# Selecting a head's decays with all 128 rows, and a new order of the mixer's attention products in a tick

## What is computed

```python
a_cs = jnp.cumsum(ac, axis=-1)
decay_in = jnp.exp(segsum(ac))
y_diag = jnp.einsum('bclgs,bgrcls,bcsgrp->bclgrp', cb, decay_in, xc)
```

```python
logits = jnp.einsum('bqhd,bkhd->bhqk', qi, k).astype(jnp.float32) * scale
logits = logits + ci.transpose(0, 2, 1)[..., None] - c_k[:, :, None, :]
logits = jnp.where(causal[None, None], logits, NEG_INF)
p = jax.nn.softmax(logits, axis=-1)
return jnp.einsum('bhqk,bkhd->bqhd', p.astype(v.dtype), v)
```

## Time and profile before

| | us |
|---|---|
| median of 3 runs | 2444.68 |
| lowest and highest | 2444.25, 2448.4 |
| the profiled execution, its own time | 2445.11 |
| its span | 2443.3 |
| TensorE busy (share of the span) | 2412.1 (99%) |
| VectorE, ScalarE, GpSimd busy | 1367.6, 1004.5, 403.0 |

### The profile page before, as it was taken

One profiled execution on the slowest core, in us unless ns is written; L12 is line 12 of the kernel. 1 busy time (PEld: TensorE's weight loads), 2 busy tenths in 40 slices (PEclk: granted clock), 3 DMA queues, 4 the chain that ended last, 5 costly groups with the idle time before them and its releaser, 6 DMA issues.

```text
span 2443.3 us, 30351 instructions
## 1 busy us (share of the span) xinstructions
PE 2412.1 (99%) x11930; PEld 1959.0 (80%) x11930; DVE 1367.6 (56%) x2158; ACT 1004.5 (41%) x1723; POOL 403.0 (16%) x320
## 2 busy tenths in 40 slices
PE   8899999999999999999999999999999999999998
PEld 6677877888888887788888877787788887888887
DVE  6868875763665455576456547534555445443342
ACT  5554553442444444454234334323443334332223
POOL 0342342210112222131001100001220001110011
PEclk9999999999999999999999999999999999999999
DMA  4542222223223221133332232231244322223222
GB/s 161 107 92 78 79 69 96 95 87 112 95 83 116 70 70 48 45 122 96 91 101 92 90 121 82 76 102 57 65 126 134 113 95 87 95 87 104 99 82 87
DMA packets 74269, 226.23 MB, mean 93 GB/s; under 512 B 8080, under 2 KB 12304, under 8 KB 74000
## 3 DMA queue, kind: packets, MB, share of 16 engines
q1 hardware_dynamic: 69696, 215.90, 27.5%
q10 hardware_dynamic: 4432, 8.39, 2.0%
HBM read 215.87 MB, written 8.39 MB: 92 GB/s over the span
## 4 chain that ended last, share of the span: by engine, by line
PE 59%; issue 0%; DVE 0%; ACT 0%; POOL 0%; POOLq 0%; DVEq 0%
PE bank L1142 58%; PE bank L1146 1%; ACT t L1536 0%; DVE t L1986 0%; DVE t L1993 0%; DVE t L1989 0%; ACT t L1539 0%; POOL t L2547 0%; POOLq L2768 0%; DVEq L2768 0%; DVE t L2469 0%; DVE t L2475 0%; POOLq L765 0%
## 5 line engine op out<-in xcount | busy, mean ns | idle before, releaser
L1142 PE MATMUL bank<-t 128*128 128x512 f32 (+4 forms) x11412 | 2381.7, 374 | 21.1 <-DVE t L1986 10.2
L1142 PEld LDWEIGHTS bank<-t 128*128 128x128 f32 (+1 forms) x11412 | 1903.7, 185 | 458.0 <-issue 91.1
L1536 ACT ACTIVATE t<-t 128x1024 fp32r<-128x1024 f32 (+5 forms) x649 | 549.6, 856 | 680.2 <-PE bank L1142 275.6
L1986 DVE TENSOR_TENSOR t<-t 128x1024 fp32r<-128x1024 f32 (+6 forms) x686 | 627.6, 925 | 252.3 <-ACT t L1536 247.3
L2547 POOL TENSOR_TENSOR t<-t 128x512 f32<-128x512 f32 (+5 forms) x240 | 362.4, 1516 | 1641.1 <-ACT t L1539 541.9
L1986 DVE TENSOR_TENSOR t<-bank,t 128x512 f32<-128x512 f32 (+4 forms) x410 | 275.4, 676 | 494.8 <-PE bank L1142 476.9
L1539 ACT ACTIVATE t<-t 128x512 f32<-128x512 f32 (+5 forms) x545 | 330.7, 616 | 522.3 <-DVE t L1986 330.0
L1989 DVE SCALAR_TENSOR_TENSOR t<-t 128x512 f32<-128x512 f32 (+6 forms) x430 | 319.5, 749 | 94.4 <-ACT t L1539 53.9
L1536 ACT ACTIVATE t<-bank 128x512 f32<-128x512 f32 (+4 forms) x150 | 71.5, 493 | 129.2 <-PE bank L1146 89.4
L2550 POOL TENSOR_SCALAR t<-t 128x128 f32<-128x128 f32 (+3 forms) x64 | 40.0, 630 | 387.5 <-ACT t L1536 252.7
L1146 PE MATMUL bank<-t 128*128 128x128 f32 x518 | 81.3, 274 | 2.1 <-ACT t L1536 1.0
(11 more groups left out here) (25 smaller groups left out, 48.5 us busy)
## 6 DMA issues: line engine op xcount, KB each, us to landing
t<-in_w SPq DMA_DIRECT2D x304, 512.0 KB, 3.4
t<-in_w SPq DMA_DIRECT2D x48, 384.0 KB, 3.0
t<-in_w SPq DMA_DIRECT2D x56, 320.0 KB, 2.9
t<-in_w SPq DMA_DIRECT2D x28, 256.0 KB, 3.1
tab<-t ACTq DMA_DIRECT2D x1, 2560.0 KB
t<-in_x SPq DMA_DIRECT2D x8, 256.0 KB, 5.0
t<-tab SPq DMA_DIRECT2D x8, 256.0 KB, 3.8
spill<-t ACTq DMA_DIRECT2D x1, 2048.0 KB, 8.4
```

Of the source, the lines that this page charges most:

```text
L1142: return eng.matmul(out, lhs, rhs, start=start, stop=stop, skip_group_check=loose)
L1536: return eng.activation(out, in_, ACT.Copy, scale=scale)
L1986: return eng.tensor_tensor(out, a, b, o)
```

## The change

It has three parts.

1. The third and fourth block of `identr` are taken from an off-diagonal block of the identity, which is zero, so column h has a 1 only in rows h and 32 + h. The selectors of both heads use all 128 rows of `identr` and of `csT` (or `cT`).
2. In the windowed attention the loops are split: all `sqk`, then all `so`, then all `sat`.
3. In the forget-gate attention: `ck`, then all `fo`, then all `fqk` with their masks, then all `fat`.

No step changes its tick. The diff, with the moved loops cut to their heads where nothing in them changes:

```diff
@@ ssm
-                rows = slice(64 * k, 64 * k + 64)
-                sel = buf.identr[rows, h:h + 1].to_broadcast([64, P])
-                mm(bank[:, :], sel, buf.csT[rows, :]).then_inc(*fill((f"s{k}", g, p)))
+                sel = buf.identr[:, h:h + 1].to_broadcast([P, P])
+                mm(bank[:, :], sel, buf.csT[:, :]).then_inc(*fill((f"s{k}", g, p)))
@@ mix
-            for tile in at("swa", T - 4 * i - 6):
...
-                t.then_inc(*fill(("sat", tile, i)))
+        for i in range(NT):
             for tile in at("swa", T - 4 * i - 8):
...
+        for i in range(NT):
+            n = (2 if i else 1) * P
+            for tile in at("swa", T - 4 * i - 6):
...
+                t.then_inc(*fill(("sat", tile, i)))
         for tile in at("fox", T):
             for half in range(2):
                 h = 2 * tile + half
                 bank = take(("ck", h))
-                rows = slice(64 * half, 64 * half + 64)
-                sel = buf.identr[rows, h:h + 1].to_broadcast([64, P])
+                sel = buf.identr[:, h:h + 1].to_broadcast([P, P])
                 w.wait_ge(*empty(("f3",)))
-                mm(bank[:, :], sel, buf.cT[rows, :]).then_inc(*fill(("ck", h)))
+                mm(bank[:, :], sel, buf.cT[:, :]).then_inc(*fill(("ck", h)))
+        for i in range(NT):
+            for tile in at("fox", T - 4 * i - 10):
+                bank = take(("fo", tile)) if i == 0 else K.of(("fo", tile))
+                w.wait_ge(*empty(("fat", tile, i, 0)))
+                w.wait_ge(*empty(("fat", tile, i, 1)))
...
         for i in range(NT):
             n = (i + 1) * P
             for tile in at("fox", T - 4 * i - 2):
...
+        for i in range(NT):
             for tile in at("fox", T - 4 * i - 8):
...
-            for tile in at("fox", T - 4 * i - 10):
...
@@ prepare
         for r in range(0, P, 32):
-            t = eng.tensor_copy(buf.identr[r:r + 32, :], buf.ident[r:r + 32, r:r + 32])
+            one = r if r < 64 else 0
+            t = eng.tensor_copy(buf.identr[r:r + 32, :], buf.ident[r:r + 32, one:one + 32])
```

More of the change, by code:

```diff
@@ L1395, in mix @@
                 t.then_inc(*(fill(("so", tile)) if i == NT - 1 else sig["av"].up("so", tile, i)))
+        for i in range(NT):
+            n = (2 if i else 1) * P
+            for tile in at("swa", T - 4 * i - 6):
+                L = buf.Lm[(4 * tile + i) % 5]
+                bank = take(("sat", tile, i))
+                for half in range(2):
+                    w.wait_ge(*sig["pn"].at("s", tile, i, half))
+                    for j in range(n // P):
+                        at_ = 256 * half + j * P
+                        t = turn(bank[:, at_:at_ + P], L[:, at_:at_ + P])
+                t.then_inc(*fill(("sat", tile, i)))
         for tile in at("fox", T):
@@ L1399, in mix @@
                 bank = take(("ck", h))
-                rows = slice(64 * half, 64 * half + 64)
-                sel = buf.identr[rows, h:h + 1].to_broadcast([64, P])
+                sel = buf.identr[:, h:h + 1].to_broadcast([P, P])
                 w.wait_ge(*empty(("f3",)))
-                mm(bank[:, :], sel, buf.cT[rows, :]).then_inc(*fill(("ck", h)))
+                mm(bank[:, :], sel, buf.cT[:, :]).then_inc(*fill(("ck", h)))
[4 more added lines that the diff above has]
+                w.wait_ge(*empty(("fat", tile, i, 1)))
+                w.wait_ge(*empty(("fv", tile // 2, 1)))
+                for j in range(i + 1):
+                    for half, rows in enumerate(halves):
+                        h = 2 * tile + half
+                        L = buf.Lm[2 * ((4 * tile + i) % 4) + half]
+                        t = mm(bank[rows, i * P:i * P + P], buf.Vb[:, j, 64 * h:64 * h + 64], L[:, j * P:j * P + P],
+                               start=j == 0, stop=j == i)
+                t.then_inc(*(fill(("fo", tile)) if i == NT - 1 else sig["av"].up("fo", tile, i)))
         for i in range(NT):
```

## The result

| | before | after |
|---|---|---|
| median of 22 runs each, us | 2444.72 | 2441.78 |
| lowest and highest | 2442.16, 2449.62 | 2440.41, 2446.28 |
| the profiled execution, its own time | 2445.11 | 2440.41 |
| its span | 2443.3 | 2438.6 |

The ratio of the times is 0.9987, 95% interval 0.9981 to 0.9993: 0.13% faster, 2.9 us between the medians, "within 0.2%" as forecast. The predicted 2440.8 us was 1.0 us too low, and the range held.

The account below looks back on a forecast made before the run. TensorE (PE) bounds the kernel, its time the sum of distances between product starts; 2.8 (state-space) + 0.5 (mixer selectors) + 0.9 (forget-gate order) - 0.3 = 3.9 us off 2445.11 gives 2441.2, median 0.43 lower: 2440.8, range 2438.8 to 2443.4.

Parts of the forecast that it names:

- a free-standing pair: State-space stage, two half-row selectors among products with no wait: full-height selectors cut 1.08 us to 0.92, gain 0.16.
- a forget-gate tick where nothing waits: Mixer's forget-gate attention, six reordered ticks: one return to the full shape fewer, 0.145 us each, 0.9 in all.
- There its own 0.23 disappears in that wait ... I take 0.29: State-space pairs at 112 and 150 us, second selector waiting for its bank: gain 0.29 us each.
- Of their 0.48 I write off 0.3: First three selector pairs, ahead of the wait at 112.43 us: 0.3 of their 0.48 us gain is lost.
- the stage absorbs it: State-space stage: ACT and DVE chains set the waits, a third of 2.5 us remains (0.8), 2442.5 us; chance 12%.
- 0.33 lost at the head, 0.33 saved behind, so 0.145 stays: Forget-gate ticks of tiles 2 and 3: V products wait for ACT's copies, logits then run together; 0.145 us gain stays.
- the milder form of the rival: Forget-gate attention: V products pay for ACT's copies in three ticks, the whole 0.9 us goes, 2441.7; counted within the forecast.
- over 0.4 us late: Forget-gate attention, sign of being wrong: V products of tiles 2 and 3 start over 0.4 us late.
- The mixer's later selectors: Three mixer pairs followed by the previous tile's transposes: 0.91 us before, 0.80 after, gain 0.11 each.
- This trace agrees on the starts and not on the price: Half-row selector pairs: they start together and overlap, but 0.43 us pass, not the 0.23 of one product.
- surcharge and overlap both stay: All 20 selector pairs: full-height ones run in sequence and keep every surcharge, +4.6 us, 2449.3 us; chance 4%.
- The rival with shrinking bank waits: State-space stage: waits for banks (0.53, 0.51 + 0.27 us) go and the 0.3 returns, 1.6 us, 2439.2; chance 18%.

## Why the prediction was right, and where it wasn't

**Right.** The bound (the sum of PE's starts), the 0.16 of a free-standing pair (0.158), 0.23 for a full-height selector, zero for the windowed order, the first mixer selectors (0.16), and 0.145 for a forget-gate tick where nothing waits (0.14 to 0.19 in four of six). Verdict, range and sign follow from these.

**The sum was 3.9, and what belongs to the change in the profiles is 2.65** (0.18 at 112 us, 1.49 from there to 385 us, 0.98 in the mixer). With 0.42 from the earlier landing and 1.59 from the clock it makes the 4.7 between the two profiled executions. That 2441.2 was forecast for an execution that took 2440.4 is thus two errors that met; the medians' 2.9 us is what to compare 2.65 with. Their interval, 1.7 to 4.6 us, holds 2.65 and 3.9 alike, so the times alone could not have told that the sum was too high; the traces do.

**"There its own 0.23 disappears in that wait ... I take 0.29" failed, in its size and at one place altogether.** At 112 us the two selectors start 0.51 apart in both kernels, as ACT sets it; so far it is as forecast. But behind them the ordinary distances don't follow. PE after:

```profile
112.53 0.50 PE L1142 MATMUL bank<-t 128*128 128x512 f32 x1
...
112.87 0.38 PE L1142 MATMUL bank<-t 128*128 128x128 f32 x2
```

0.34 from the waiting selector to the next product, where I took 0.23, then 0.11. Before it was 0.42 (112.94 in the earlier trace rows to 113.37) and 0.21:

```profile
113.37 0.38 PE L1142 MATMUL bank<-t 128*128 128x128 f32 x1
...
113.58 0.39 PE L1142 MATMUL bank<-t 128*128 128x128 f32 x2
```

So 0.63 less 0.45 is 0.18, not 0.29: behind a product that waited the next pays 0.11, as behind a change of shape. At 150 us, too, the distances behind give this. But there the second selector starts when ACT has read its bank, ACT ran 0.60 ahead of before since 112 us, and PE, 0.77 ahead with one more pair's gain, waits until it is at 0.60 again (149.59 after, 150.19 in the earlier trace rows). That gives 0.02 instead of 0.29 for the place, and with the pair ahead of it 0.19 instead of 0.45.

**A wait ahead of a pair, which I didn't look for.** The places at 245 and 253 us gave 0.02 together (-0.21 and 0.23), forecast 0.32. PE before, then after:

```profile
245.53 1.83 PE L1142 MATMUL bank<-t 64*128 64x512 f32 x10 [0.30 <-ACT t L1539]
```

```profile
244.28 1.64 PE L1142 MATMUL bank<-t 128*128 128x512 f32 x9 [0.46 <-ACT t L1542]
```

The wait grew by 0.16, since PE came earlier by more than ACT did; the first selector is 1.25 ahead, after 1.41. Behind it the second selector starts 0.34 later, then 0.24 and 0.11 follow, 0.69 in all against 0.64 before. Nothing is gained behind a wait with both banks free, for the surcharge of the entry lay under it before.

**"Of their 0.48 I write off 0.3" was too little.** All 0.48 went; the wait's end is the landing of weights plus ACT's work, whatever PE does. This is a part of the rival "the stage absorbs it", whose total of 0.8 for the stage was too low: 1.67 stayed.

**The V products of tiles 2 and 3.** "0.33 lost at the head, 0.33 saved behind, so 0.145 stays": 0.04 and 0.05 stayed (selectors of before, new order). The wait came as described, but a V product starts 0.14 us behind the end of ACT's copy, while there the logits started 0.06 behind it (1705.43 less 1705.37). Of the difference this takes 0.08; the rest, a few hundredths, wasn't traced. Here the milder form of the rival was the truth in two of its three ticks. By the prediction's own sign ("over 0.4 us late") the working was wrong at this place: the V products waited 0.41 and 0.51 us, and started some 0.47 late.

**The mixer's later selectors** (forecast 0.11 each, 0.5 with the first): alone they gave 0.30 in all. In tiles 2 and 3 0.11 was gained at the selectors and then lost. The second head's transposes behind them start 0.06 behind DVE's work (1701.10 after 1701.04, and 1733.82 after 1733.76, in the kernel with the selectors alone), so PE can't come earlier there: 0.07 goes in tile 2 and all 0.11 in tile 3. The rest of tile 2, 0.05, goes a tick later, where the second half's logits wait for ACT's copy.

**"This trace agrees on the starts and not on the price" was wrong.** The 0.43 us is one product (0.23) and 0.20 of a change of shape, as the rival "surcharge and overlap both stay" put it, whose other half, that the surcharge belongs to something else than the shape, fell: with like shapes it was gone. The Trainium skill, "TensorE: Matmul & The Clock Gate", Part 3, that a pack costs about one product, holds in this case (1.08 with overlap, 1.31 without, difference 0.23). What counted against it was another rule of the Trainium skill, in "TensorEngine Tiling (Array Packing)", Key Properties: "Changing tiling mode (not just tile) drains the TensorE". The trace agrees that a change of shape costs time, at each change 0.09 us on the first product; that these 0.09 are the drain is the reading of the Trainium skill, which no view here shows. The 0.11 on the second product, for weights not loaded ahead, that rule doesn't name. The 0.32 on the way in and the 0.33 behind the first full product, both in the same rows as the 0.43, would have told it: 0.09 of the one and 0.11 of the other are just what 0.43 has over 0.23.

**Range and chances.** The rival with shrinking bank waits (18%) was wrong in sign: at 112 us the wait doubled, from 0.53 to 1.11. Its price of 1.6 us was too high by its own rows, too: 0.51 and 0.27 are distances between two selectors, and 0.23 of each stays without any wait.

## What to carry to other kernels

Small products side by side save a product's time, but only if the array is in that shape anyway: among full-size products of 512 columns each change of shape costs 0.2 us, so one pair (0.40 paid, 0.23 saved) loses; by these numbers two pairs in a row would about break even (an estimate, not run). A product saved ahead of a wait is worth nothing when the wait ends by another engine or a transfer, so add up gains wait by wait, including waits that stand ahead of the edited place. For effects of a few tenths of a per cent, align the starts of like products in two traces and take out the stretches at a lower clock, before believing a difference of two times.

## What was new about the hardware

- One product of 64 rows among products of 128 rows costs 0.40 us more than one of 128 rows (0.33, 0.42 and 0.34 against 0.23 each).
- Weights of the next product are loaded ahead within one shape, and not across a change of it: the load then begins with the product itself, after 0.36 us without loads. Behind a full-size product that had waited for its bank the next one was 0.11 us late too (0.34 instead of 0.23, at 112, 150 and 245 us).
- Loads of 512 KB took 17.5 us in the median (of three) beside a store of 2560 KB and 4.4 us where only half of that store had been issued.
- After the same wait of 1.97 us PE sometimes runs at 1.2 GHz for some 3.5 us and sometimes not, in the same kernel. It costs 1.4 to 1.6 us each time, half the effect of this change.
